# Three fp32r passes per product become one plain fp32 product, and four loading slots become ten

## Chip, cores, metric

The kernel runs on one core of one Trainium2 chip. The time is the device time in microseconds of one execution; the median of three runs stands below. One execution was also profiled. Engines are named as in the profile: PE (matrix products) with PEld (its weight loads), DVE (vector), ACT (activations), POOL, and SP, which here issues the weight transfers.

## What is computed

Two transformer-like blocks over 16 + 256 tokens of width 1024, everything in fp32. The first block has two layers:

```python
h = concat(meta_tokens, x)                              # 272 x 1024
h = layer_norm(ALPHA * h + rglru_block(h, ...))         # recurrent block, width 1344, gates 8 x 168 x 168
h = layer_norm(ALPHA * h + swiglu(h, ffn_w_in, ffn_w_out))     # 1024 -> 2 x 3584 -> 1024
h = layer_norm(ALPHA * h + gla_block(h, ...))           # gated linear attention, 4 heads
h = layer_norm(ALPHA * h + moe_swiglu(h, ...))          # top 2 of 8 experts, D_FF 3584
```

The last 256 rows go on to a second block: a modulation by a vector through `w_ada_2` (1024 x 6144), a mixed latent and differential attention (projections `w_in_2`, `w_uq_2`, `w_ukv_2`, `w_o_2`), and a mixture of 16 experts of width 512.

## The kernel before, in words

Each engine has one program, written out in order; semaphores count what is done, and a `wait_ge` names the mark. PE, ACT, DVE, POOL and SP go through: setup, recurrent block (`pe_rg`, L867), FFN (`pe_ffn`, L1107), GLA (`pe_gla`, L1256), router and first mixture (`pe_first`), second attention (`pe_mid`, L2755), router and second mixture (`pe_pairs`).

All weights outside the mixtures come in chunks of up to 128 x 2048 fp32 (1 MB), listed in a `Stream` named M in the order of use: 105 chunks before the first mixture, 16 after it. `load_chunks` (L483, issued by SP) puts chunk i into raw slot i mod 4. Most chunks are then *split*: ACT writes the part that fp32r keeps (`split_hi`, L454, the instruction at L462), DVE subtracts it from the raw chunk (`split_lo`, L474, at L480), into one of three pairs of slots. A raw slot is free again once its chunk is split (or, for chunks that PE also reads raw, used); a pair is free once PE has used it. The 24 chunks of `w_ada_2` are not split. The programs of ACT and DVE call the splits by hand, between their other work, in the order of the chunks.

Activations that are the other operand are turned by PE (transposes into PSUM) and are split too: `act_turn` and `dve_turn` (L511, L521), and where a layer norm's gain and shift belong to it, `act_shift_turn` and `dve_shift_turn` (L533, L548), which first write the value to a temporary tile, then its high part, then its low part. The key names which turn: x0, x1, x2, x3, x5, cq, x6, x6b. In the recurrent block the convolution's result and y are split in the same way (xch, xcl), in the FFN the gated value (fah, fal). A bank of PSUM goes back when the low part is written.

Every product of this kind is `mm3`:

```python
e.matmul(o, lh, rh, start=start, stop=False)     # L437
e.matmul(o, lh, rl, start=False, stop=False)     # L438
return e.matmul(o, ll, rh, start=False, stop=stop)   # L439
```

It is called in the recurrent block (`pe_rg_in`, the gates, the output), in the FFN (gate and up with the weights stationary and 272 columns streamed; down with the activations stationary and 512 columns streamed), in GLA through `pe_chan`, `pe_tokm`, `pe_rows_out` and `pe_last_two` (L1222, L1232, L1244, L642), and in `pe_mid`. Products with a raw operand are plain fp32 already: the modulation (`pe_ada`), the 16 meta rows of the down and output products (`pe_meta_rows`), GLA's small products (L1274 is one of four with 272 columns), attention, and the experts' products of both mixtures.

Both mixtures load expert weights into a ring in the memory that raw, high and low slots (10 together) held before, plus one slot (first) or three (second). `ring_slots` (L1558) gives for each slot the mark after which it is free. `load_first` (L1585) reads the expert's number from the tile perm, which the routing writes, before it issues the first load. The second mixture's order is fixed. `load_chunks` for the 16 chunks of the second attention waits until the first mixture's last use of the slot.

Of the kernel before, what the change touches and what calls it, by code (L numbers as in the profile page):

```python
# [18 lines left out]
T = 272  # L19
CW = 2048  # L20
NRAW, NSPL = 4, 3
# [98 lines left out]
class Stream:  # L120


    def __init__(self, raw, hi, lo, pe, name=""):
        self.raw, self.hi, self.lo, self.pe, self.name = raw, hi, lo, pe, name
        self.chunks, self.split, self.index, self.stop, self.kept = [], [], {}, None, set()

    def add(self, key, rows, n, pieces, split=True, zero=False, keep=False):
        i = len(self.chunks)
        if keep:
            self.kept.add(i)  # L130
        if split:
            self.split.append(i)
        self.index[key] = i
        self.chunks.append((key, rows, n, pieces, len(self.split) - 1 if split else None, zero))

    def again(self):
        for sig in (*self.raw, *((self.hi, self.lo) if self.hi is not None else ())):
            sig.n = 0


def build(nc, d, out):
# [9 lines left out]
    M = Stream([Sig(sem(f"s_raw{i}_in")) for i in range(NRAW)], Sig(sem("s_hi")), Sig(sem("s_lo")), pe)  # L151
# [4 lines left out]
    with ExitStack() as own:  # L156
        right = lambda name, shape, dt=F32: own.enter_context(nc.sbuf_tensor(name, shape, dt, side="right"))
        xh = right("xh", [128, 8, T], F32R)
        xl = right("xl", [128, 8, T], F32R)
        raw = right("raw", [128, NRAW, CW])  # L160
        whi = right("whi", [128, NSPL, CW], F32R)
        wlo = right("wlo", [128, NSPL, CW], F32R)
    with ExitStack() as own:
        xg1_ = own.enter_context(nc.sbuf_tensor("xg1", [128, 2560], F32, side="right"))
# [3 lines left out]
    ring = right("ring", [128, NRAW + 2 * NSPL, CW])  # L168
# [31 lines left out]
    def plan_ada(n):  # L200

        for _ in range(n):
            j = next(n_ada)
            part = w_ada[256 * (j % 4):256 * (j % 4) + 256, 1024 * (j // 4):1024 * (j // 4) + 1024]
            M.add(("ada", j), 128, CW, by_rows(part, 0, 2, 1024), split=False)

# [15 lines left out]
    for j in range(6):  # L222
        M.add(("ro", j), 112, CW, by_blocks(w_ro, j, 112), keep=True)
# [5 lines left out]
    for j in range(14):  # L229
        M.add(("ffn", "d", j), 128, CW, by_blocks(d["ffn_w_out"][0], j, 128), keep=True)  # L230
# [19 lines left out]
    def plan_first(S, key):  # L250
# [4 lines left out]
        def chunk(x, u, nm, gi, j):  # L255
# [9 lines left out]
            S.add((key, x, nm, gi, j, u), 128, w, pieces, split=False)  # L265
# [9 lines left out]
    first_split = len(M.split)  # L275
# [10 lines left out]
    def plan_pairs(S, key):  # L286

        rows_of = lambda w, j, m: (lambda s: [(s.rearrange("p (k n) -> p k n", k=m), w.rearrange("(p k) n -> p k n", p=128)[:, j * m:j * m + m, :])])
        for what, x in moe_order(8, 512):
            for nm, n in (("g", "w_gate_2"), ("u", "w_up_2")) if what == "u" else (("d", "w_down_2"),):  # L290
                for j in range(2):
                    for u in range(2):
                        S.add((key, x, nm, j, u), 128, CW, rows_of(d[n][0, 2 * x + u], j, 2 if nm == "d" else 4), split=False)

    R1 = Stream([Sig(sem(f"s_first{i}_in")) for i in range(NRING1)], None, None, pe, "first")
    plan_first(R1, "m1")
    R2 = Stream([Sig(sem(f"s_ring{i}_in")) for i in range(NRING)], None, None, pe, "second")
# [3 lines left out]
    class Again:  # L301


        def __init__(self, name, n_ring, plan, keys):
            self.pe, self.act, self.dve = (Sig(sem(f"s_{name}_{n}_done")) for n in ("pe", "act", "dve"))
            self.S = Stream([Sig(sem(f"s_{name}_ring{i}_in")) for i in range(n_ring)], None, None, self.pe, name)
# [38 lines left out]
    xch = ph("xch", [112, 12, T], F32R)  # L345
    xcl = ph("xcl", [112, 12, T], F32R)
# [4 lines left out]
    fah = ph("fah", [128, 28, T], F32R)  # L351
    fal = ph("fal", [128, 28, T], F32R)
    fam = ph("fam", [128, 28, 32])
# [51 lines left out]
    cq = ph("cq", [128, 2, 5, 256], F32R)  # L405
# [30 lines left out]
    def mm3(e, o, lh, ll, rh, rl, start, stop):  # L436
        e.matmul(o, lh, rh, start=start, stop=False)  # L437
        e.matmul(o, lh, rl, start=False, stop=False)  # L438
        return e.matmul(o, ll, rh, start=False, stop=stop)  # L439

    def weights(e, S, key):

        i = S.index[key]
        _, rows, n, _, s, _ = S.chunks[i]
        if s is None:
            e.wait_ge(S.raw[i % NRAW].s, S.raw[i % NRAW].at(i))
            return raw[0:rows, i % NRAW, 0:n]
        e.wait_ge(S.lo.s, S.lo.at(s))
        return whi[0:rows, s % NSPL, 0:n], wlo[0:rows, s % NSPL, 0:n]
# [4 lines left out]
    def split_hi(e, S, s):  # L454
        if s >= (len(S.split) if S.stop is None else S.stop):
            return
        i = S.split[s]
        _, rows, n, _, _, _ = S.chunks[i]
        e.wait_ge(S.raw[i % NRAW].s, S.raw[i % NRAW].at(i))
        if s >= NSPL:  # L460
            e.wait_ge(S.pe.s, S.pe.at("used", S.split[s - NSPL]))
        e.activation(whi[0:rows, s % NSPL, 0:n], raw[0:rows, i % NRAW, 0:n], ACT.Copy).then_inc(S.hi.s, S.hi.up((s,)))  # L462

    def split_half(e, S, s, half):
        i = S.split[s]
        a = slice(CW // 2 * half, CW // 2 * half + CW // 2)
        e.wait_ge(S.hi.s, S.hi.at(s))
        ins = e.tensor_tensor(wlo[:, s % NSPL, a], raw[:, i % NRAW, a], whi[:, s % NSPL, a].bitcast(F32), ALU.subtract)
        if half:
            ins.then_inc(S.lo.s, S.lo.up((s,)))  # L470
        else:
            ins.then_inc(dve.s, dve.up())

    def split_lo(e, S, s):  # L474
        if s >= (len(S.split) if S.stop is None else S.stop):
            return
        i = S.split[s]
        _, rows, n, _, _, _ = S.chunks[i]
        e.wait_ge(S.hi.s, S.hi.at(s))
        e.tensor_tensor(wlo[0:rows, s % NSPL, 0:n], raw[0:rows, i % NRAW, 0:n], whi[0:rows, s % NSPL, 0:n].bitcast(F32),  # L480
                        ALU.subtract).then_inc(S.lo.s, S.lo.up((s,)))

    def load_chunks(e, S, begin, end):  # L483

        for i in range(begin, end):
            _, rows, n, pieces, s, zero = S.chunks[i]
            k = i % NRAW
            if first <= i < first + NRAW:
                e.wait_ge(pe.s, pe.at("ring", R1.name, last_in(ring[:, 2 * NSPL + k, :])))
            if i >= NRAW:  # L490
                p = S.chunks[i - NRAW][4]
                if p is None or i - NRAW in S.kept:
                    e.wait_ge(S.pe.s, S.pe.at("used", i - NRAW))
                else:
# [3 lines left out]
            slot = raw[0:rows, k, 0:n]  # L498
# [4 lines left out]
    def pe_turn(e, key, src, tiles, nk):  # L503
        for k in range(nk):
# [4 lines left out]
            bank.give((key, k), (dve, key, "lo", k))  # L509

    def act_turn(e, key, tiles, nk, hi, gain=None):  # L511
        c0, c1 = min(c for _, _, c in tiles), max(c + n for _, n, c in tiles)
        for k in range(nk):
            p, o = bank(key, k)[:, c0:c1], hi[:, k, c0:c1]
            e.wait_ge(pe.s, pe.at(key, "T", k))
            if gain is not None and gain(k) is not None:
                e.activation(o, p, ACT.Copy, scale=gain(k)).then_inc(act.s, act.up((key, "hi", k)))
            else:
                e.activation(o, p, ACT.Copy).then_inc(act.s, act.up((key, "hi", k)))

    def dve_turn(e, key, tiles, nk, hi, lo, gain=None):  # L521
        c0, c1 = min(c for _, _, c in tiles), max(c + n for _, n, c in tiles)
        for k in range(nk):
            p, oh, ol = bank(key, k)[:, c0:c1], hi[:, k, c0:c1], lo[:, k, c0:c1]
            e.wait_ge(act.s, act.at(key, "hi", k))
            if gain is not None and gain(k) is not None:
                e.scalar_tensor_tensor(ol, p, gain(k), oh.bitcast(F32), ALU.mult, ALU.subtract).then_inc(dve.s, dve.up((key, "lo", k)))  # L527
            else:
                e.tensor_tensor(ol, p, oh.bitcast(F32), ALU.subtract).then_inc(dve.s, dve.up((key, "lo", k)))  # L529

    NTMP = 4

    def act_shift_turn(e, key, tiles, hi, gain, shift, tmp):  # L533


        c0, c1 = min(c for _, _, c in tiles), max(c + n for _, n, c in tiles)
        for k in (1, 3, 5, 7):
            x = tmp[:, k % NTMP, 0:c1 - c0]
            e.wait_ge(pe.s, pe.at(key, "T", k))
            if k >= NTMP:  # L540
                e.wait_ge(dve.s, dve.at(key, "lo", k - NTMP))
            e.activation(x, bank(key, k)[:, c0:c1], ACT.Identity, bias=shift(k), scale=gain(k)).then_inc(act.s, act.up((key, "x", k)))
            for j in (k - 1, k):
                sig = act if j % 2 else dve
                e.wait_ge(sig.s, sig.at(key, "x", j))
                e.activation(hi[:, j, c0:c1], tmp[:, j % NTMP, 0:c1 - c0], ACT.Copy).then_inc(act.s, act.up((key, "hi", j)))

    def dve_shift_turn(e, key, tiles, hi, lo, gain, shift, tmp):  # L548
        c0, c1 = min(c for _, _, c in tiles), max(c + n for _, n, c in tiles)

        def whole(k):
            e.wait_ge(pe.s, pe.at(key, "T", k))
            if k >= NTMP:
# [2783 lines left out]
```

## Time and profile before

| | us |
|---|---|
| median of 3 runs | 1938.63 (1934.21 to 1939.75) |
| the profiled execution | 1938.98 |
| its span, first to last instruction | 1936.9 |
| PE busy in it | 1812.8 (94%) |
| DVE, ACT, POOL busy | 607.6, 476.9, 351.6 |
| mean granted PE clock | 0.964 |

A span's engines overlap, so busy times don't add up. A row of PE has the time from a record's start to its modelled end; successive records overlap, and the distance of their starts is what a record costs in a stream. The granted clock is given as a share of 2.4 GHz.

### The profile page before, as it was taken

To read this page: it belongs to the slowest core of one execution; us is meant where nothing else is said; L and a number is where in the kernel's file an instruction comes from. 1 tells how busy PE (TensorE), PEld (TensorE's weight loads), DVE (VectorE), ACT (ScalarE), POOL (GpSimd) and SP (SyncE) were. 2 spreads that over 40 slices of the span, in tenths; PEclk is the share of its full clock that TensorE was granted. 3 is DMA by queue.
4 is the path that set the end of the run, shared out by engine and by line. 5 is a ranking of instruction groups with operands and counts; after the bars stand their busy time and mean duration, and the time that the engine had idled before them with its cause. 6 is when DMAs were issued, how large, how long until landed. Compare 5 with 4: busy or idle time off the path is not lost.

```text
span 1936.9 us, 26926 instructions
## 1 busy us (share of the span) xinstructions
PE 1812.8 (94%) x11141; PEld 1033.9 (53%) x11141; DVE 607.6 (31%) x1227; ACT 476.9 (25%) x799; POOL 351.6 (18%) x306
## 2 busy tenths in 40 slices
PE   7999999999998999999999999999997887699998
PEld 7987999777975333323332333222322886544443
DVE  6777554338466200100010000000001685501112
ACT  5854444325332110000100000000001564321121
POOL 3000000000000699999930000000000000000000
PEclk9998999998998899999999999999999897889999
DMA  6555667446724999999999999999998440569997
GB/s 192 150 146 187 202 199 241 142 141 220 249 89 155 402 418 413 420 419 420 413 419 420 419 412 416 420 419 419 415 420 297 137 158 9 217 275 417 420 420 291
DMA packets 152739, 582.87 MB, mean 301 GB/s; under 512 B 11673, under 2 KB 77866, under 8 KB 109600
## 3 DMA queue, kind: packets, MB, share of 16 engines
q1 hardware_dynamic: 150000, 575.09, 76.4%
q0 software_dynamic: 2608, 5.97, 1.2%
q8 instruction: 91, 1.49, 0.3%
q14 instruction: 40, 0.33, 0.1%
HBM read 579.96 MB, written 1.05 MB: 300 GB/s over the span
## 4 chain that ended last, share of the span: by engine, by line
PE 73%; DMA 14%; DVE 8%; ACT 3%; issue 1%; SPq 0%; ACTq 0%; DVEq 0%
PE ps L1789 17%; DMA ring<-in_moe_w_out 9%; PE ps L437 9%; PE ps L438 8%; PE ps L439 8%; PE ps L2294 6%; PE ps L1782 5%; PE ps L1821 4%; PE ps L2318 3%; DMA ring<-in_moe_w_in 3%; DVE wlo L480 2%; DMA more<-in_moe_w_out 1%; PE ps L1825 1%; DMA more<-in_moe_w_in 1%; PE ps L637 1%
## 5 line engine op out<-in xcount | busy, mean ns | idle before, releaser
L1789 PE MATMUL ps<-ring,xg 128*64 128x512 f32 x1638 | 406.3, 599 | 4.5 <-DMA ring<-in_moe_w_in 2.4
L480 DVE TENSOR_TENSOR wlo<-raw,whi 128x2048 fp32r<-128x2048 f32 (+5 forms) x96 | 211.5, 2207 | 190.0 <-ACT whi L462 189.7
L1789 PEld LDWEIGHTS ps<-ring,xg 128*64 128x64 f32 x1638 | 120.9, 137 | 247.5 <-issue 239.6
L462 ACT ACTIVATE whi<-raw 128x2048 fp32r<-128x2048 f32 (+6 forms) x97 | 178.7, 1846 | 184.7 <-PE ps L439 77.5
L1821 PE MATMUL ps<-ring,ahm 128*64 128x512 f32 x808 | 203.4, 597 | 8.4 <-DMA ring<-in_moe_w_out 8.4
L437 PE MATMUL ps<-xh,whi 128*128 128x272 f32 (+1 forms) x712 | 210.6, 296 | 0.6 <-DVE xl L529 0.6
L439 PE MATMUL ps<-xh,wlo 128*128 128x272 f32 (+1 forms) x712 | 208.8, 293 | 0.0
L438 PE MATMUL ps<-xl,whi 128*128 128x272 f32 (+1 forms) x712 | 208.6, 293 | 0.0
L2219 POOL TENSOR_SCALAR lnt<-lnt,h 128x384 f32<-128x384 f32 x120 | 188.6, 1572 | 12.2
L1962 DVE TENSOR_TENSOR sgm<-sgm,ps 128x512 f32<-128x512 f32 x28 | 17.5, 683 | 495.7 <-PE ps L1789 495.7
L437 PEld LDWEIGHTS ps<-xh,whi 128*128 128x128 f32 (+1 forms) x712 | 133.7, 188 | 4.0 <-issue 2.4
L438 PEld LDWEIGHTS ps<-xl,whi 128*128 128x128 f32 (+1 forms) x712 | 133.8, 188 | 0.5
L439 PEld LDWEIGHTS ps<-xh,wlo 128*128 128x128 f32 (+1 forms) x712 | 133.5, 187 | 0.5
L1821 PEld LDWEIGHTS ps<-ring,ahm 128*64 128x64 f32 x808 | 63.4, 136 | 131.4 <-issue 131.4
L2221 POOL TENSOR_TENSOR bias<-bias,lnt 128x384 f32<-128x384 f32 x120 | 120.2, 1002 | 10.0
L437 PE MATMUL ps<-whi,xh 128*128 128x256 f32 (+3 forms) x368 | 112.2, 305 | 3.3 <-DVE xl L527 1.6
L438 PE MATMUL ps<-wlo,xh 128*128 128x256 f32 (+3 forms) x368 | 111.1, 302 | 0.0
L439 PE MATMUL ps<-whi,xl 128*128 128x256 f32 (+3 forms) x368 | 110.9, 301 | 0.0
L1782 PE MATMUL ps<-ring,xg 128*32 128x384 f32 (+1 forms) x936 | 106.4, 554 | 2.7 <-DMA ring<-in_moe_w_in 2.3
L2294 PE MATMUL ps<-ring,xg 128*64 128x512 f32 x392 | 100.0, 608 | 1.6 <-ACT xg L2358 1.6
L2517 POOL DMA_DIRECT2D gbr<-in_mla_q_g x1 | 0.5, 547 | 511.4 <-ACT kk L2721 511.4
L1972 DVE SCALAR_TENSOR_TENSOR yl<-ps,gs,yh 128x512 fp32r<-128x512 f32 x8 | 5.6, 747 | 271.0 <-ACT yh L1910 271.0
(586 smaller groups left out, 2439.8 us busy)
## 6 DMA issues: line engine op xcount, KB each, us to landing
ring<-in_moe_w_in SPq DMA_DIRECT2D x117, 1024.0 KB, 19.6
ring<-in_moe_w_out SPq DMA_DIRECT2D x101, 1024.0 KB, 20.1
ring<-in_moe_w_in SPq DMA_DIRECT2D x117, 768.0 KB, 11.9
ring<-in_w_gate SPq DMA_DIRECT2D x29, 1024.0 KB, 14.2
raw<-in_ffn_w_in SPq DMA_DIRECT2D x28, 1024.0 KB
ring<-in_w_down SPq DMA_DIRECT2D x26, 1024.0 KB, 12.9
raw<-in_w_ada SPq DMA_DIRECT2D x24, 1024.0 KB
ring<-in_w_up SPq DMA_DIRECT2D x20, 1024.0 KB, 9.9
```

The costliest lines, as they stand in the source:

```text
L437: e.matmul(o, lh, rh, start=start, stop=False)
L438: e.matmul(o, lh, rl, start=False, stop=False)
L439: return e.matmul(o, ll, rh, start=False, stop=stop)
L462: e.activation(whi[0:rows, s % NSPL, 0:n], raw[0:rows, i % NRAW, 0:n], ACT.Copy).then_inc(S.hi.s, S.hi.up((s,)))
L480: e.tensor_tensor(wlo[0:rows, s % NSPL, 0:n], raw[0:rows, i % NRAW, 0:n], whi[0:rows, s % NSPL, 0:n].bitcast(F32), ALU.subtract).then_inc( ...
L1782: ins = e.matmul(po[32 * c:32 * c + 32, 0:n // 4], a[:, j, 128:160], quarter(both[0][:, 0, :], n, c), start=j == 0, stop=j == 7)
L1789: ins = e.matmul(ps_[b][64 * v:64 * v + 64, :], a[:, j, 64 * v:64 * v + 64], both[v][:, 0, 512 * b:512 * b + 512], start=j == 0, stop=j == 7)
L1821: ins = e.matmul(D[q][64 * v:64 * v + 64, :], w["ahm"][:, f, 64 * v:64 * v + 64], both[v][:, i, 512 * q:512 * q + 512], start=f == 0, stop ...
L2219: e.tensor_scalar(stp[:, :], rel[:, :], float(th), dl[:, i, hh:hh + 1], ALU.is_ge, ALU.mult).then_inc(pool.s, pool.up())
L2221: e.tensor_tensor(bias[:, hh, :], bias[:, hh, :], stp[:, :], ALU.add).then_inc(pool.s, pool.up())
L2294: ins = e.matmul(p[64 * v:64 * v + 64, :], xg[:, kk_, u + 64 * v:u + 64 * v + 64], both[v][:, k, :], start=kk_ == 0, stop=kk_ == 7)
L2318: ins = e.matmul(D[q][64 * v:64 * v + 64, :], w["ah"][:, x % 2, f, 64 * v:64 * v + 64], both[v][:, i, 512 * q:512 * q + 512], start=f == 0 ...
```

## The change

`mm3`, `split_hi`, `split_lo`, `split_half` and the shift turns are gone. Every product that was `mm3` is one `e.matmul` on fp32 tiles; the chunks are used where they land. The stream M has ten slots (the ring's own) in place of four; a slot is free when PE has used its chunk. xh is the tile xg, xl is gone; cq, fa, X2 and I are used unsplit. A turn is shared: DVE writes the even k, ACT the odd, each in one instruction with gain and shift, and a bank goes back at that mark. `ring_slots` takes an order of the last ten chunks. POOL's four memsets for the gates' chunks wait for nothing. The router's products, the mixtures and the attention inside are as they were.

```diff
-NRAW, NSPL = 4, 3
+NRAW = 10
...
-    ring = right("ring", [128, NRAW + 2 * NSPL, CW])
+    ring = right("ring", [128, NRAW, CW])
+    xh = xg
...
     def load_chunks(e, S, begin, end):
...
             if first <= i < first + NRAW:
-                e.wait_ge(pe.s, pe.at("ring", R1.name, last_in(ring[:, 2 * NSPL + k, :])))
+                e.wait_ge(pe.s, pe.at("ring", R1.name, last_in(ring[:, k, :])))
             if i >= NRAW:
-                p = S.chunks[i - NRAW][4]
-                if p is None or i - NRAW in S.kept:
-                    e.wait_ge(S.pe.s, S.pe.at("used", i - NRAW))
-                else:
-                    e.wait_ge(S.lo.s, S.lo.at(p))
+                e.wait_ge(S.pe.s, S.pe.at("used", i - NRAW))
...
+    def dve_turn(e, key, tiles, nk, to, gain=None, shift=None):
         c0, c1 = min(c for _, _, c in tiles), max(c + n for _, n, c in tiles)
+        for k in range(0, nk, 2):
+            p, o = bank(key, k)[:, c0:c1], to[:, k, c0:c1]
+            e.wait_ge(pe.s, pe.at(key, "T", k))
+            if shift is not None:
+                e.tensor_scalar(o, p, gain(k), shift(k), ALU.mult, ALU.add).then_inc(dve.s, dve.up((key, "x", k)))
...
                     for k in range(8):
                         if j == 0 and nm == "g" and i == 0:
-                            e.wait_ge(dve.s, dve.at("x1", "lo", k))
-                        ins = mm3(e, p, wh[:, k, 128 * i:128 * i + 128], wl[:, k, 128 * i:128 * i + 128], xh[:, k, :], xl[:, k, :],
-                                  k == 0, k == 7)
+                            wait_x(e, "x1", k)
+                        ins = e.matmul(p, w[:, k, 128 * i:128 * i + 128], xh[:, k, :], start=k == 0, stop=k == 7)
...
-                e.tensor_tensor(g, g, bank("fu", f)[:, 0:T], ALU.mult).then_inc(dve.s, dve.up(("fu", f)))
-                e.wait_ge(act.s, act.at("fa", f))
-                e.tensor_tensor(fal[:, f, :], g, fah[:, f, :].bitcast(F32), ALU.subtract).then_inc(dve.s, dve.up())
-                e.tensor_copy(fam[:, f, :], g[:, 0:32]).then_inc(dve.s, dve.up(("fa", f)))
+                e.tensor_tensor(fa[:, f, :], g, bank("fu", f)[:, 0:T], ALU.mult).then_inc(dve.s, dve.up(("fu", f), ("fa", f)))
...
+    LAST1 = chunk_at(*(("ada", j) for j in (16, 17, 18)), ("go", 2), ("go", 3), *(("ada", j) for j in range(19, 24)))
+    LAST2 = list(range(len(M.chunks) - NRAW, len(M.chunks)))
+    SLOTS1 = ring_slots(LAST1, [more1[:, i, :] for i in range(NMORE1)], "end_gla")
```

## Rows read from the trace of the kernel before

**Rows 1.** The page, chain of waits by engine, whole span
```profile
PE 73%; DMA 14%; DVE 8%; ACT 3%; issue 1%; SPq 0%; ACTq 0%; DVEq 0%
```

**Rows 2.** Windows by stage: us, busy (instructions) of each engine, PEclk, DMA share, GB/s
```profile
0.00:620.00 620.00, 592.19 (x4337) 514.53 (x4337) 367.86 (x618) 270.40 (x354) 23.28 (x38) 0.97 0.55 179
620.00:1500.00 880.00, 832.84 (x4631) 274.85 (x4632) 72.65 (x209) 60.17 (x122) 320.64 (x257) 0.98 1.00 408
1500.00:1702.00 202.00, 160.08 (x1009) 144.43 (x1007) 133.09 (x337) 100.37 (x220) 7.67 (x12) 0.84 0.38 125
1702.00:1936.90 234.90, 227.70 (x1166) 100.14 (x1166) 34.01 (x66) 45.96 (x106) 0.00 (x0) 0.99 0.91 376
```

**Rows 3.** Groups of PE by form, line L437 (busy us, mean ns)
```profile
L437 PE MATMUL ps<-xh,whi 128*128 128x272 f32 x512 | 151.1, 295 | 0.0
...
L437 PE MATMUL ps<-whi,xh 128*128 128x256 f32 x256 | 72.5, 283 | 0.9 <-ACT row L613 0.9
...
L437 PE MATMUL ps<-xh,whi 128*112 128x272 f32 x192 | 56.3, 293 | 0.6 <-DVE xl L529 0.6
...
L437 PE MATMUL ps<-whi,fah 128*128 128x512 f32 x112 | 45.4, 405 | 0.0
...
L437 PE MATMUL ps<-whi,xh 128*128 128x512 f32 x64 | 26.2, 410 | 1.8 <-DVE xl L527 1.6 <-DVE xl L529 0.2
...
L437 PE MATMUL ps<-whi,xch 112*128 112x512 f32 x48 | 19.4, 404 | 0.0
...
L437 PE MATMUL ps<-xch,whi 112*112 112x272 f32 x56 | 17.0, 303 | 2.2 <-ACT R L928 2.2
```

**Rows 4.** PE timeline at three places: start us, duration us
```profile
299.91 0.29 PE L437 MATMUL ps<-xh,whi 128*128 128x272 f32 x1
...
301.81 0.29 PE L437 MATMUL ps<-xh,whi 128*128 128x272 f32 x1
...
539.91 0.27 PE L437 MATMUL ps<-whi,xh 128*128 128x256 f32 x1
...
541.33 0.28 PE L437 MATMUL ps<-whi,xh 128*128 128x256 f32 x1
...
149.86 0.39 PE L437 MATMUL ps<-whi,xch 112*128 112x512 f32 x1
...
151.24 0.39 PE L437 MATMUL ps<-whi,xch 112*128 112x512 f32 x1
```

**Rows 5.** Plain fp32: source line L1274; then weight loads of L2274, timeline
```profile
L1274 PE MATMUL ps<-zT,h x8: 387/388/463, 461.4 to 463.0; 16*128 16x272 f32 x8
...
1816.12 0.19 PEld L2274 LDWEIGHTS ps<-h,cst 128*128 128x128 f32 x1 [0.24 <-issue]
...
1818.27 0.19 PEld L2274 LDWEIGHTS ps<-h,cst 128*128 128x128 f32 x1 [0.24 <-issue]
```

**Rows 6.** Window of the gates stage, columns as in rows 2
```profile
56.10:80.90 24.80, 22.64 (x168) 22.41 (x168) 18.73 (x42) 19.11 (x32) 0.00 (x0) 0.93 0.42 120
```

**Rows 7.** Who PE waited for: us in total, times, longest us
```profile
PE ps L437 <- DVE wlo L480: 4.1, 2, 3.5
...
PE ps L2637 <- ACT Sx L2629: 2.8, 2, 2.5
...
PE ps L437 <- ACT R L928: 2.2, 1, 2.2
...
PE ps L730 <- DVE xl L560: 1.7, 2, 0.8
```

**Rows 8.** DVE timeline before the first softmax
```profile
1589.78 4.49 DVE L480 TENSOR_TENSOR wlo<-raw,whi 128x2048 fp32r<-128x2048 f32 x2
```

**Rows 9.** SP's queue, 600 to 640 us
```profile
624.96 6.21 SPq L1601 DMA_DIRECT2D ring<-in_moe_w_in  x10
```

**Rows 10.** PE timeline, GLA's outputs: start us, us, records
```profile
557.03 0.70 PE L1323 MATMUL ps<-vt,sc 128*128 128x256 f32 x2
557.66 0.65 PE L1325 MATMUL ps<-Sst,E 128*64 128x256 f32 x4
```

More of the change, by code:

```diff
@@ L120, with __init__, add @@
 class Stream:
[L123 to L134, printed above, removed]
+    def __init__(self, raw, pe, name=""):
+        self.raw, self.pe, self.name = raw, pe, name
+        self.chunks, self.index = [], {}
+    def add(self, key, rows, n, pieces, zero=False):
+        self.index[key] = len(self.chunks)
+        self.chunks.append((key, rows, n, pieces, zero))
     def again(self):
-        for sig in (*self.raw, *((self.hi, self.lo) if self.hi is not None else ())):
+        for sig in self.raw:
             sig.n = 0
@@ L150, in build @@
         "posr", "relb", "small", "br", "out")}
-    M = Stream([Sig(sem(f"s_raw{i}_in")) for i in range(NRAW)], Sig(sem("s_hi")), Sig(sem("s_lo")), pe)
+    M = Stream([Sig(sem(f"s_raw{i}_in")) for i in range(NRAW)], pe)
     cst = sb("cst", [128, C_END])
[L156 to L162, printed above, removed]
     with ExitStack() as own:
@@ L433, in build @@
     phase_ctx[0].close()
[L436 to L439, printed above, removed]
     def weights(e, S, key):
         i = S.index[key]
[L444 to L449, printed above, removed]
+        _, rows, n, _, _ = S.chunks[i]
@@ L451, in used @@
+        e.wait_ge(S.raw[i % NRAW].s, S.raw[i % NRAW].at(i))
+        return ring[0:rows, i % NRAW, 0:n]
     def used(S, key):
         return ("used", S.index[key])
[L454 to L470, printed above, removed]
-        else:
[L472 to L481, printed above, removed]
@@ L496, in load_chunks @@
             if zero:
                 e.wait_ge(pool.s, pool.at("zero", i))
-            slot = raw[0:rows, k, 0:n]
+            slot = ring[0:rows, k, 0:n]
             for dst, src in pieces(slot):
@@ L508, in pe_turn, with act_turn @@
             ins.then_inc(pe.s, pe.up((key, "T", k)))
-            bank.give((key, k), (dve, key, "lo", k))
-    def act_turn(e, key, tiles, nk, hi, gain=None):
+            bank.give((key, k), by_turns(key, k))
+    def act_turn(e, key, tiles, nk, to, gain=None, shift=None):
         c0, c1 = min(c for _, _, c in tiles), max(c + n for _, n, c in tiles)
-        for k in range(nk):
-            p, o = bank(key, k)[:, c0:c1], hi[:, k, c0:c1]
+        for k in range(1, nk, 2):
+            p, o = bank(key, k)[:, c0:c1], to[:, k, c0:c1]
@@ L531, in build @@
[L531 to L546, printed above, removed]
@@ L709, in by_turns, with wait_x, pe_turn_tiles @@
         return (act if k % 2 else dve, key, "x", k)
-    def act_router_turn(e, key, gain, shift):
-        for k in range(1, 8, 2):
-            e.wait_ge(pe.s, pe.at(key, "T", k))
-            e.activation(xg[:, k, 0:256], bank(key, k)[:, 0:256], ACT.Identity, bias=shift(k), scale=gain(k)).then_inc(
-                act.s, act.up((key, "x", k)))
-    def dve_router_turn(e, key, gain, shift):
-        for k in range(0, 8, 2):
-            e.wait_ge(pe.s, pe.at(key, "T", k))
-            e.tensor_scalar(xg[:, k, 0:256], bank(key, k)[:, 0:256], gain(k), shift(k), ALU.mult, ALU.add).then_inc(
-                dve.s, dve.up((key, "x", k)))
-    def pe_turn_tiles(e, key, norm, tiles, nk, ahead, back=None):
+    def wait_x(e, key, k):
+        sig, *mark = by_turns(key, k)
+        e.wait_ge(sig.s, sig.at(*mark))
+    def pe_turn_tiles(e, key, norm, tiles, nk, ahead):
         p = {}
@@ L741, in pe_turn_tiles @@
             e.transpose(p[k][:, c:c + n], src_h(t, k), idn[0:n, 0:n]).then_inc(pe.s, pe.up((key, "T", k)))
-            bank.give((key, k), (dve, key, "lo", k) if back is None else back(key, k))
+            bank.give((key, k), by_turns(key, k))
     def pool_ln(e, i, *after):
@@ L798, in pool_setup @@
             i = M.index["gt", j]
-            p = M.chunks[i - NRAW][4]
-            if p is None:
-                e.wait_ge(pe.s, pe.at("used", i - NRAW))
-            else:
-                e.wait_ge(M.lo.s, M.lo.at(p))
-            e.memset(raw[0:112, i % NRAW, 0:2016], 0.0).then_inc(pool.s, pool.up(("zero", i)))
+            e.memset(ring[0:112, i % NRAW, 0:2016], 0.0).then_inc(pool.s, pool.up(("zero", i)))
     def pe_setup(e):
@@ L1153, in act_ffn @@
         for j in range(14):
-            for _ in range(2):
-                split_hi(e, M, s)
-                s += 1
             for f in (2 * j, 2 * j + 1):
@@ L1179, in dve_ffn @@
         for j in range(14):
-            for _ in range(2):
-                split_lo(e, M, s)
-                s += 1
             for f in (2 * j, 2 * j + 1):
@@ L1470, in dve_gla @@
         dve_ada(e, 3)
-        for j in range(6):
-            split_lo(e, M, s)
-            s += 1
         for ch in range(4):
@@ L2223, in pool_rel @@
         pool.label(("round_m1",))
-    SLOTS = ring_slots("wo", len(M.chunks), [more[:, i, :] for i in range(2)], "end_mid") + [(xslot[:, 0:CW], ((pe, "m2", "logits"),))]
+    SLOTS = ring_slots(LAST2, [more[:, i, :] for i in range(2)], "end_mid") + [(xslot[:, 0:CW], ((pe, "m2", "logits"),))]
     NP = 8
@@ L2772, in pe_mid @@
                 for k in range(3):
[L2773 removed]
+                    ins = e.matmul(p[:, 0:384], cq[:, k, cc:cc + 128], w[:, k, :], start=k == 0, stop=k == 2)
                 ins.then_inc(pe.s, pe.up(("uq", j, t), used(M, ("uq", j))))
                 bank.give(("uq", j, t), (act, "uq", j, t))
[L2776 removed]
+        w = weights(e, M, ("ukv", 0)).rearrange("p (k n) -> p k n", k=2)
         for t, _, cc in QTILES:
@@ L3039, in dve_mid @@
         dve_angles(e)
-        for j in range(3):
-            split_lo(e, M, s)
-            s += 1
         for t in range(2):
```

417 lines of the change are left out of this document (105 added, 312 removed).

## The prediction

> **What bounds the kernel now.** I read first the chain of waits: PE carries 73% of it and the DMA 14% [rows 1], so PE is the first suspect. The windows by stage [rows 2] then say where. Up to 620 us (recurrent block, first FFN, GLA) PE is busy 592.2 of 620 us at a mean clock of 0.97, while the DMA stands at 0.55, DVE at 368 us and ACT at 270 us: this stage is PE's, and splitting is beside it. From 620 to 1500 (first mixture) the DMA share is 1.00 at 408 GB/s: that stage is the DMA's. From 1500 to 1702 (second attention) PE is busy 160 of 202 us at clock 0.84: a stage of handovers between engines. The second mixture follows. The edited products lie in the first and third window only, and there PE's own rate is what the edit changes.
>
> **Counts.** A product of three passes is one record each at L437, L438 and L439. The forms of L437 [rows 3] give 512 + 192 + 56 products that stream 272 columns and 8 more for gz, so 768; 256 that stream 256 columns, and by the code 32 more with a 16-wide stationary tile (gv, tile 2); 112 + 64 + 48 that stream 512, and by the code 8 more (ukv), so 232; by the code 12 of 384 columns (uq) and 16 of 160 (wi 8).
>
> **The price of a pass now.** Durations overlap, so I take starts, not durations. 272 columns: from 299.91 to 301.81 there are 15 steps of 0.127 us; 256: from 539.91 to 541.33, 12 steps of 0.118; 512: from 149.86 to 151.24, 6 steps of 0.230 [rows 4]. A product costs three: 0.380, 0.354 and 0.690 us.
>
> **The price of a plain fp32 product.** The trace has some. At L1274 the code has four products of 272 columns and the row has 8 records: a plain product is two records. They start in 1.6 us for 7 steps, 0.229 each. At L2274, with a full 128x128 stationary tile and 512 columns, the weight loads start from 1816.12 to 1818.27 in 5 steps of 0.430 [rows 5]. Between the two it is 0.84 ns per column, 2 cycles of 2.4 GHz; so 256 columns give 0.216 and 384 give 0.322 per record. A plain product then costs 0.458 (272), 0.432 (256), 0.860 (512). It is one third fewer records, but each streams at half the rate.
>
> The Trainium skill, "FP8 and Floating Point Precision", TensorE Precision Notes, says that true fp32 takes four passes through the array, a reduced read of fp32 one. The trace agrees: 0.860 us for 512 columns is 4.03 cycles per column. A second rule speaks louder against the change: "TensorE: Matmul & The Clock Gate", Back-to-back issue gap, gives columns/2.4 + 2.5 ns for a pass, which would be 116 ns for 272 columns where the trace has 127. By it the three passes would cost 0.347, 0.328 and 0.648 us and the added PE time would be some 164 us in place of the 123 below. Of the passes that run now the measurement decides.
>
> **Added on PE.** 768 x 0.078 = 59.9; 288 x 0.078 = 22.5; 232 x 0.170 = 39.4; 12 of 384 columns, interpolated, 12 x 0.12 = 1.5; the 16 of 160 columns: bounds -1 (by columns) and +1 (the 256-column difference), taken as 0. Sum +123.3 us. It falls in stages where PE is the limit, so all of it is on the path, unless waits disappear.
>
> **What comes off.**
> - The splits themselves (L462 on ACT, L480 on DVE) and the second half of every turned operand: beside PE's work nearly everywhere (DVE busy 368 of 620 us), so worth only the waits below.
> - Gates, 56.1 to 80.9: 168 records at 0.127 would take 21.3, the stretch took 24.8 [rows 6]; ACT came late there behind splits (PE waited 2.2 for ACT R L928 [rows 7]). Minus 3.5.
> - x1 and x2: PE waited 1.7 us in two waits for DVE xl L560, which gives banks back [rows 7]; now the turned value itself does. Minus 1.7. What ends these turns next is the norm itself (DVE, then ACT), which stays.
> - ukv: PE waited 3.5 us for DVE wlo L480 [rows 7]; with ten slots its weights lie ready. Minus 3.5, and minus 1.8 because those 24 records then run warm: between 0, if they stay cold, and 1.8.
> - Attention: two splits held DVE 4.49 us from 1589.78 [rows 8], just before the first softmax; ACT's two are similar. Bounds 0 (if PE's scores end later anyway) and 4.5. PE's longest wait for the softmax (ACT Sx L2629) was 2.5 [rows 7]; ACT's backlog delays the heads' copies before it too, so I take minus 3.7, nearer to the upper end. What is late next is ACT's row of exponentials.
> - The low halves of x at the first product, at x6b and at the x3 turn, and ACT's ada rows late behind splits: minus 3.6 together, between 0 and 5 (an estimate: four to five handovers like the two of x1 and x2, at 0.85 each).
> - Against it: where the granted clock is 1.2 GHz a pass of 272 columns takes 272/1.2 = 0.227, and the difference of a product is one pass, 0.227, not 0.078. Bounds 0 and 5 (ten such stretches, half a microsecond each), taken as 2.
>
> Sum of these: -3.5 - 1.7 - 5.3 - 3.7 - 3.6 + 2 = -15.8.
>
> **Ten loading slots.** In the first stage a 1 MB chunk feeds 16 products, 7.3 us after the change, at a DMA share of 0.55 now: no wait to win. The ring's first expert loads are issued at 624.96 [rows 9], after the routing's perm (load_first reads it), in both kernels; free slots earlier change nothing. After the first mixture the first loads of the second block now wait for the last two expert chunks, since slot 5 is the one used next to last; PE then has a norm to wait for and eight transposes ahead of wi 0, a product set of 16 lasts 6.9 us (16 x 0.432), and a chunk of 1 MB lands each 2.6 us at 408 GB/s [rows 2]: cost 0, and 5 at the most, two chunks' landing. The 13 slots of the second mixture come free before it in both kernels, the last at the router's logits: 0. POOL's memsets lose a wait and hold nobody. The 0.078 per product also delays nothing else: DVE, ACT and SP follow PE here.
>
> **Forecast.** Span 1936.9, the execution 1938.98, so 2.1 us lie around the span. 1938.98 + 123.3 - 15.8 = 2046.5; the median of the runs is 1938.63, 0.3 lower. I say **2046 us**, about 5.5% slower.
>
> **Rivals.**
> - *Weight loads come out from behind the streams.* At L1323 two plain records of 256 columns take 0.63 us until the next line starts, 0.315 each where 0.216 was priced: 0.10 more [rows 10]. If every new record paid that, 2 x 1316 x 0.10 = +263, so 2310. It decides as soon as a load cannot start under the stream before it. Against it: at L2274 six loads of the same size are hidden in a stream, and L1323 alternates with 64-wide tiles. If the plain streams only carry the excess that the passes of 272 have over their columns (127 against 113, so 14 ns), it is 2632 x 0.014 = +37: 2083. Chance 0.06 for the small form, 0.02 for the full one.
> - *Faster: a plain record streams as a pass does.* Two records of 0.127 in place of three: 768 x 0.127 + 288 x 0.118 + 232 x 0.23 = -185, with the waits about 1740. It decides below a record of 1.5 passes, 0.190 us for 272 columns. Rows 5 speak against it with 0.229 measured; only a difference between these few products and the new ones could save it. Chance 0.02.
> - *PE's longer stage is hidden by the DMA.* The expert loads would have to start before 620; up to 11 chunks of 2.6 us are 28 us, which gives 2018. Rows 9 and the read of perm speak against it. Chance 0.03.
> - *The waits hold more than I took off.* PE's idle time up to 620 is 28 us and in the third window 42 [rows 2], most of it norms and softmax. If another 15 go: 2031. Inside the forecast's range. Chance of the forecast with this: 0.87.
>
> **Range and chances.** 2028 takes in all bounds of waits (another 8) and half of the last rival; 2068 takes in no gain from attention and ukv (+9), the cold bound (+3) and a third of the 14 ns excess. About 0.3% is what a measurement of this kernel can tell from no change. Faster comes from the second rival, 0.02; same has no mechanism of its own, a partial sum of several, 0.01; slower 0.97.
>
> **What would show it.** Right: one matmul line in place of three, with two records per product; starts 0.229 apart at 272 columns and 0.43 at 512; the FFN's gate and up part (448 products) about 35 us longer, the window of the first mixture 880 us as before, only later; no PE wait on ukv. Wrong: spacings over 0.24 at 272 columns, PE waits on DMA for weights before 620, expert loads issued before the routing, or a first mixture that is shorter.

## The result and the profile after

The changed kernel takes **2036.73 us** (median of 4 runs, 2034.33 to 2038.59) where the kernel before takes 1937.86 beside it: a ratio of 1.0512, 95% interval 1.0492 to 1.0531, or 99 us more. The forecast was 2046, range 2028 to 2068. The direction and its cause, dearer products on the engine that sets the pace, hold. The 99 are not made of the terms that I summed, though: I had +123.3 on PE and -15.8 beside it, and the profiled spans differ by 95.3 (1936.9 and 2032.2), so some 28 us came back, not 15.8.

The page of the changed kernel, busy time by engine and the chain of waits by engine (before: [rows 1]):

```profile
PE 1923.1 (95%) x9825; PEld 971.9 (48%) x9825; DVE 363.3 (18%) x1011; ACT 279.9 (14%) x611; POOL 350.2 (17%) x306
...
PE 81%; DMA 13%; DVE 4%; ACT 1%; issue 1%; SPq 0%; ACTq 0%; DVEq 0%
```

PE carries 81% of the chain instead of 73%; DVE falls from 8% to 4%. The windows of the changed kernel, columns as in [rows 2], here cut at the changed kernel's own stage ends (first stage, first mixture, second attention, and the gates alone):

```profile
0.00:703.00 703.00, 683.40 (x3099) 460.85 (x3099) 150.73 (x395) 98.00 (x187) 23.00 (x38) 0.98 0.49 157
703.00:1582.00 879.00, 838.61 (x4721) 275.79 (x4720) 74.42 (x224) 60.26 (x118) 316.48 (x250) 0.98 0.98 403
1582.00:1798.00 216.00, 173.92 (x840) 135.36 (x840) 104.18 (x326) 75.75 (x201) 10.71 (x18) 0.89 0.41 137
63.16:88.83 25.67, 25.67 (x113) 19.82 (x112) 8.54 (x32) 13.26 (x26) 0.00 (x0) 1.00 0.52 154
```

The whole loss is in the first window. The same two instructions, the first record of GLA's last ada rows ahead of the routing, start at 606.56 before and at 703.10 after, 96.5 us apart; the end of the last mixture's records moves by 95.3. The mixture only starts later, and in the second attention, where the products add some 18 us (128 x 0.078, 40 x 0.17 and 1.5), nearly all of it is given back.

The price of a plain product, from the critical chain of the changed kernel (start us, us, what; each row is one unbroken series of records):

```profile
239.37 29.44 PE ps L921 x128
269.81 29.53 PE ps L921 x128
...
506.41 13.95 PE ps L561 x32
...
574.39 21.20 PE ps L1020 x96
```

L921 (FFN gate and up, 272 columns), L561 (512) and L1020 (256) are the priced forms. With the last record's own duration taken off (0.395, 0.595 and 0.382 us, the means of their groups) the steps are (29.53 - 0.395) / 127 = 0.229, 13.36 / 31 = 0.431 and 20.82 / 95 = 0.219 us. I had priced 0.229, 0.430 and 0.216 from eight records and six weight loads of another part of the kernel [rows 5].

Who PE waited for, changed kernel (us in total, times, longest us):

```profile
PE ps L450 <- ACT hn L2273: 9.5, 1, 9.5
...
PE ps L638 <- ACT h L609: 6.2, 3, 2.6
...
PE ps L2377 <- ACT Sx L2369: 1.0, 3, 0.4
```

No wait on split weights is left, since there are none. Ahead of the x1, x2 and router turns (L638) PE now waits for the norm instead of for banks.

### The profile page after: what moved, and what is told of

It is laid out like the page before. It is cut to its first block, busy times and chain, and to the rows that moved or that the text cites. A ratio compares the mean times of both kernels' runs of the same rounds, so it can differ in the third digit from the quotient of the medians.

```text
span 2032.2 us, 23789 instructions
## 1 busy us (share of the span) xinstructions
PE 1923.1 (95%) x9825; PEld 971.9 (48%) x9825; DVE 363.3 (18%) x1011; ACT 279.9 (14%) x611; POOL 350.2 (17%) x306
## 4 chain that ended last, share of the span: by engine, by line
PE 81%; DMA 13%; DVE 4%; ACT 1%; issue 1%; SPq 0%; ACTq 0%; DVEq 0%
PE ps L1533 16%; PE ps L921 10%; DMA ring<-in_moe_w_out 9%; PE ps L1020 6%; PE ps L2037 6%; PE ps L1565 4%; PE ps L745 4%; PE ps L1526 4%; PE ps L942 4%; PE ps L2061 3%; PE ps L561 3%; DMA ring<-in_moe_w_in 3%; PE ps L1008 2%; PE ps L776 1%; PE ps L761 1%; PE ps L1569 1%
## 5 line engine op out<-in xcount | busy, mean ns | idle before, releaser
L921 PE MATMUL ps<-xg,ring 128*128 128x272 f32 x896 | 208.5, 395 | 0.0
L921 PEld LDWEIGHTS ps<-xg,ring 128*128 128x128 f32 x896 | 170.5, 191 | 36.9 <-issue 2.1
L1020 PE MATMUL ps<-ring,xg 128*128 128x256 f32 (+2 forms) x608 | 131.6, 377 | 0.0
L1020 PEld LDWEIGHTS ps<-ring,xg 128*128 128x128 f32 (+1 forms) x608 | 107.8, 181 | 23.3 <-issue 3.2
L745 PE MATMUL ps<-xg,ring 128*112 128x272 f32 x384 | 90.6, 399 | 0.0
L942 PE MATMUL ps<-ring,fa 128*128 128x512 f32 x192 | 85.6, 599 | 0.0
L745 PEld LDWEIGHTS ps<-xg,ring 128*112 128x112 f32 x384 | 69.2, 181 | 20.7
L1533 PE MATMUL ps<-more,xg 128*64 128x512 f32 x154 | 70.5, 597 | 1.2 <-DVE sgm L1706 0.9
L1569 PE MATMUL ps<-ring,aho 128*32 128x512 f32 x400 | 52.4, 602 | 5.5 <-DMA ring<-in_moe_w_out 4.1
L942 PEld LDWEIGHTS ps<-ring,fa 128*128 128x128 f32 x192 | 35.5, 190 | 45.1 <-issue 45.1
```

The costliest lines, as they stand in the source:

```text
L745: ins = e.matmul(p, w[:, k, 112 * i:112 * i + 112], xh[:, k, :], start=k == 0, stop=k == 7)
L921: ins = e.matmul(p, w[:, k, 128 * i:128 * i + 128], xh[:, k, :], start=k == 0, stop=k == 7)
L942: e.matmul(acc[t, q][0:n, :], fa[:, f, cc:cc + n], w[:, i, 512 * q:512 * q + 512], start=f == 0, stop=False)
L1020: ins = e.matmul(p, xh[:, k, cc:cc + nt], w[:, k, :], start=k == 0, stop=k == 7)
L1533: ins = e.matmul(ps_[b][64 * v:64 * v + 64, :], a[:, j, 64 * v:64 * v + 64], both[v][:, 0, 512 * b:512 * b + 512], start=j == 0, stop=j == 7)
L1569: ins = e.matmul(Do[32 * c:32 * c + 32, :], w["aho"][:, 2 * j + i, :], both[0][:, i, 512 * q:512 * q + 512], start=j == 0, stop=j == 13)
```

## The experiments

Each ran beside the kernel before; ratios are to it. Spans quoted are those of the profiled executions.

**1. Plain products, but every split kept.** From the kernel before:

```diff
     def mm3(e, o, lh, ll, rh, rl, start, stop):
-        e.matmul(o, lh, rh, start=start, stop=False)
-        e.matmul(o, lh, rl, start=False, stop=False)
-        return e.matmul(o, ll, rh, start=False, stop=stop)
+        return e.matmul(o, lh.bitcast(F32), rh.bitcast(F32), start=start, stop=stop)
```

> The kernel before, its splits, its four loading slots and all their waits kept, but each product is one plain fp32 product of the two high parts (both products with a low part are left out, so less is computed). Theory (the passes cost +123 us on PE, and what the change gives back comes from the splits alone): the passes' +123 us stay whole, and most of the 28 us that the change gave back stay out, so 1938 + 123 = 2061 us, or down to 2050 where slower products cover some split waits. Rival (the 28 us come from PE itself, as from a better clock, or from the slots): the same 2037 us as the changed kernel if from the product's form, since the splits cost nothing.

Measured: 2044.94 us, 1.0576 (1.0558 to 1.0593); span 2040.5. Below my theory's range (2050 to 2061) and above the rival's value (2037). Taking away all the splitting, sharing the turns and adding six slots is worth together the 8.3 us between its span and the changed kernel's. So of some 28 us that come back, about 20 come back with every split still in place. The gates show how (window of the gates in this run):

```profile
64.57:90.32 25.75, 25.75 (x114) 19.74 (x113) 17.45 (x38) 19.06 (x32) 0.00 (x0) 1.00 0.43 135
```

ACT still works 19.06 us here, as before [rows 6], and PE no longer waits: it takes 25.75 us with the splits and 25.67 without. It was not the splits' going that removed this wait. PE became slower than what it had waited for. The clock is part of it too: 1.00 in this window, 0.93 before [rows 6]. Of the wait on split weights (3.5 us ahead of ukv in [rows 7]) only 0.8 us is left, although each weight is still split.

**2. Fewer slots filled ahead.** The changed kernel with the loads held back, to six, seven or eight chunks:

```diff
             if i >= NRAW:
-                e.wait_ge(S.pe.s, S.pe.at("used", i - NRAW))
+                e.wait_ge(S.pe.s, S.pe.at("used", i - 6))
```

> The changed kernel, but each load waits until the chunk six places earlier has been used, so that at most six of the ten slots are filled ahead. Theory (the number of slots brings nothing: a 1 MB chunk feeds PE for 3.5 us or more and 2.6 us suffice to land one): 2037 us, within 1.5 us. Rival (the ten slots carry part of the 28 us that the change gave back): slower by 3 us or more, with PE waiting for the ring's loads in the dense stages.

Measured: 2046.95 us, 1.0575 (1.0555 to 1.0595). My theory fell: slots matter. The row for it, from who PE waited for:

```profile
PE ps L509 <- DMA ring<-in_w_ada: 10.4, 4, 4.8
```

All four waits lie in one place, at the end of GLA, where the stream has five chunks of w_ada close together and PE takes 1.9 us for each. Held back to four chunks the program stops, each engine waiting for another, so there is no time for that; where the circle closes was not looked into. To see whether the kernel before would have been as short of slots (it had four raw and three split ones), seven and eight:

> The changed kernel with loads at most seven chunks ahead (four loading slots plus three split ones were seven). With six, PE waited 10.4 us for w_ada chunks of the ring around 660 to 710 us, where five of them follow each other and PE needs only 1.9 us for each. Theory A (the kernel before had enough depth for this run of short chunks, so the ten slots bring nothing over it): 2037 to 2039 us, without those waits. Theory B (each slot less costs one landing in that run of chunks): 2041 to 2044 us, some 5 to 8 us of waits for w_ada left.

> The changed kernel with loads at most eight chunks ahead. Theory A: as with ten, 2037 us. Theory B: 2038 to 2041 us, between seven and ten.

Measured: seven 2043.96 us, 1.0554 (1.0538 to 1.0570), with this row:

```profile
PE ps L509 <- DMA ring<-in_w_ada: 4.7, 2, 3.5
```

Eight: 2040.43 us, 1.0539 (1.0523 to 1.0555), one such wait of 2.6 us. Both medians agree with theory B. In the traces the first part of the first mixture starts 10.7 (six), 7.6 (seven) and 4.0 us (eight) later than with ten. SP's queue in this stretch suggests why. First the kernel with seven, 650 to 730 us (who the queue waited for), then its issues of w_ada (start us, us, count) and, last, those of run 1 in its own stretch:

```profile
SPq L443 <- PE ps L561: 14.5, 1, 14.5
```

```profile
664.93 39.21 SPq L443 DMA_DIRECT2D ring<-in_w_ada  x6
```

```profile
658.53 51.09 SPq L498 DMA_DIRECT2D raw<-in_w_ada  x7
```

Without splits a loading slot is held until the last product of its chunk, and L561 reads two chunks of go for 14 us. With seven slots one load of w_ada stands 14.5 us behind it. The kernel before needed no more than seven, since its split freed the raw slot before PE read the copy (lines 491 to 495 wait for the split). That last step is read from the code, not shown by a run. In run 1, too, one load of w_ada stands 14.5 us behind a wait for PE, without making PE wait. What the traces do show is that PE has no wait on w_ada, neither in the kernel before nor in run 1, both with four raw slots and three pairs. So ten slots gain nothing over the kernel before, but they are part of the price of taking the split away: with seven in all, the change costs 7 us more.

**3. Two splits moved.** The kernel before, three passes, with the second and third wo chunk split after the first softmax step, not ahead of it (DVE's half; ACT's likewise):

```diff
-        for _ in range(2):
-            split_lo(e, M, s)
-            s += 1
         dve_scores(e, 0)
...
         dve_scores(e, 2)
+        split_lo(e, M, s)
         dve_values(e, 0)
...
         dve_probs(e, 2)
+        split_lo(e, M, s + 1)
+        s += 2
         dve_values(e, 2)
```

> The kernel before, three passes kept; only the splits of the second and third chunk of wo are moved out of the time before the first softmax: ACT's after the second group's head copies and before the last group's exponentials, DVE's before the first and the third group's value sums. Theory (the attention gave back 7.9 us because these four splits stood ahead of the softmax): 4 to 8 us faster than the kernel before, 1930 to 1934 us, with the stretch from the last of wi to the first product of wo shorter by that. Rival (PE's other waits, or the slower head copies, set that stretch): 1938 us, within 1 us; or slower, if the later splits now delay the value sums or wo.

Measured: 1932.12 us, 0.9979 (0.9967 to 0.9991), 3 to 4 us less than before: the right way, at the lower edge of the 4 to 8 expected. Its twelve runs lie between 1926.76 and 1936.21 us, and the time goes with the mean granted clock of the run: the three at 0.964 took 1934.8 to 1935.8, the four at 0.969 took 1926.8 to 1929.0. The profiled one took 1935.32. The chain of the kernel before (start us, us) shows what was moved, with what stood on DVE's path up to the softmax:

```profile
1581.85 2.20 DVE wlo L480
1584.05 2.27 DVE rs L3074 x2
...
1588.56 1.22 DVE pj L3080
1589.87 4.40 DVE wlo L480 x2
1594.27 2.61 DVE Sx L2618 x8
1596.90 1.82 DVE ssum L2622 x2
1598.75 1.04 ACT Sx L2629 x5
```

From the first head turn to wo's first product the kernel before takes 1641.13 - 1585.53 = 55.60 us, this one 49.67, so 5.9 less (2.2 of it is lost again between GLA and the x5 turn, in the first mixture above all); the changed kernel takes 47.76, 7.8 less. But run 1, with all splits where they were, takes 46.85, less than any of them. Something else is in that stretch. The starts of the same instructions, in us after the first head turn, and the mean granted clock from it to wo, show where:

| | first transpose of exponentials | first value product | next scores | wo | clock |
|---|---|---|---|---|---|
| before | 14.35 | 23.79 | 31.50 | 55.60 | 0.79 |
| experiment 3 | 10.09 | 18.69 | 25.60 | 49.67 | 0.87 |
| changed kernel | 10.10 | 18.69 | 25.77 | 47.76 | 0.89 |
| run 1 | 11.76 | 20.36 | 24.40 | 46.85 | 0.96 |

Up to the first value product, moving the splits and having none are worth the same. Run 1 keeps them and is ahead of the kernel before by 2.6 us at the first transpose: the slower products already cover part of the splits. After the value products it overtakes the others. The granted clock is the difference there: windows of PE (us, busy, clock, DMA share, GB/s) around those 24 value products and the 12 transposes behind them, in the kernel before, the changed kernel and run 1:

```profile
1609.32:1617.10 7.78, 7.78 (x39) 0.50 0.00 0
```

```profile
1705.39:1712.54 7.15, 7.15 (x40) 0.55 0.00 0
```

```profile
1713.53:1717.64 4.11, 4.11 (x40) 1.00 0.00 0
```

In the kernel before PE worked only 6.5 of the 10 us from 1590 on, behind the softmax; from 1600 on its clock was 0.60 and then 0.50, which is 1.2 GHz:

```profile
1590.00:1600.00 10.00, 6.50 (x41) 1.00 0.59 209
1600.00:1605.00 5.00, 4.10 (x20) 0.60 0.02 5
1605.00:1610.00 5.00, 4.21 (x22) 0.50 0.00 0
```

Those records, on the path, ran at that level before, nearly all of them in the changed kernel too, and at 2.4 GHz in run 1. Why the clock stayed up in run 1 is not shown: PE worked 3.29 and 2.80 us of the two stretches of 5 us from 1705 on, no more than the 3.19 and 2.81 us of those from 1598 on in experiment 3, where the clock then fell.

**4. PE kept busy where it waits.** Experiment 3 with transposes of the identity ahead of PE's waits in the attention, into banks that the next product overwrites (they add nothing to any result):

```diff
+    def fill(e, p, n):
+        for _ in range(n):
+            e.transpose(p[:, 0:128], idn, idn)
...
         bk = [bank.take(e, "values", B, t) for t in range(2)]
+        fill(e, bk[0], (0, 0, 36, 18)[B])
```

> The kernel with the two moved wo splits, and transposes of the identity added where PE idles in the attention (3 ahead of each score product of the second group, 5 ahead of each of the first group's transposes of the exponentials, 16 ahead of the last group's head turns, 36 and 18 ahead of the third and the last group's value products), into banks that the next product overwrites. Theory (in the run that kept the splits but had single plain products, the attention came out 5 us shorter from the first exponentials to the x6 turn than in the kernel before, because its granted clock stayed at 1.00 where that of the others fell to 0.50): the clock stays high from 1600 to 1640, and the kernel comes out 3 to 8 us below the one with moved splits, 1924 to 1929 us. Rival (the clock falls anyway, or the softmax on ACT and DVE sets every step and hides the cold products): within 1 us of it, or some tenths slower by the added transposes.

Measured: 1925.42 us, 0.9944 (0.9928 to 0.9961). PE's windows of experiment 3 and of this one:

```profile
1590.00:1640.00 50.00, 38.86 (x257) 0.86 0.15 49
```

```profile
1590.00:1640.00 50.00, 47.41 (x371) 1.00 0.13 43
```

The clock stays at 1.00 and the stretch from the first head turn to wo falls to 45.22 us, another 4.4, although the added transposes delay its first value product by 1.7 us (20.44 after the first head turn, 18.69 in experiment 3). So the clock was that second thing. The median is 6.7 us below experiment 3's; the 2.3 beyond this stretch lie in parts that were not edited. In the profiled executions 1.1 of it stands at the x7 turn, where the clock came out higher; the rest has no cause shown. The Trainium skill, "TensorE: Matmul & The Clock Gate", Part 1: The HAM clock gate, says that the engine runs at half its clock after it has idled and at the full one once it is kept busy; here the clock fell behind idle time in experiment 3 and held at 1.00 once PE was kept busy, and work without a use will do. Run 1, idle as much before its value products and at 1.00, shows that idle time does not always bring it down.

**5. The same at the other long waits**: ahead of the gates, of the x1, x2, x3, x5 and x7 turns and of ukv.

```diff
+        p0 = bank.take(e, "ukv", 0, 0)
+        fill(e, p0, 30)
         wh, wl = (w.rearrange("p (k n) -> p k n", k=2) for w in weights(e, M, ("ukv", 0)))
```

> The kernel of the run e5_warm (three passes, moved wo splits, PE kept busy in the attention) with transposes of the identity also where PE waits ahead of the gates, of the x1, x2, x3, x5 and x7 turns and of ukv. In e5_warm the granted clock was below 0.9 at 166 to 176, 449 to 459, 578 to 584, 1497 to 1518 and 1557 to 1563 us, some 45 us in all of which PE was busy for about 35 and on the path for about 25. Theory (cold products on the path cost up to their warm time again): 6 to 13 us below e5_warm, 1912 to 1919 us, with a granted clock of 1.00 there. Rival (the norms on ACT and DVE set the turns, and the added transposes delay what they stand ahead of): within 2 us of e5_warm, to either side.

Measured: **1920.05 us, 0.9915 (0.9902 to 0.9929)**, 16 us below the kernel before and some 116 below the changed one, with the arithmetic of three passes unchanged. That is 5 us better than run 4, just short of the 6 to 13 expected. At x1 the clock rose only in part:

```profile
160.00:178.00 18.00, 13.88 (x70) 0.72 0.83 289
```

```profile
160.00:178.00 18.00, 15.98 (x105) 0.91 0.82 289
```

(run 4, then this one). The turn itself took 9.63 us from the last product before it to the first one behind it in both, since the norm on ACT and DVE sets when PE may go on; 1.0 us came from the products behind it. The gates gave 1.5, ukv 1.6, the x7 turn 1.1. Ahead of x5 the clock stood at 0.90 instead of 0.66 and 1.3 us came of it.

**6. Two passes.** The kernel before without its third product (low part of the left operand by high part of the right one):

```diff
         e.matmul(o, lh, rh, start=start, stop=False)
-        e.matmul(o, lh, rl, start=False, stop=False)
-        return e.matmul(o, ll, rh, start=False, stop=stop)
+        return e.matmul(o, lh, rl, start=False, stop=stop)
```

> The kernel before with the third product (low part of the left operand by the high part of the right one) left out, all splits, slots and waits kept. Theory (PE bounds the dense stages, DVE and ACT follow at half their time): one pass comes off each of some 1300 products, 768 x 0.127 + 288 x 0.118 + 232 x 0.230 + 12 x 0.17 = 187 us, of which new split and load waits give back 10 to 40: 1760 to 1790 us. Rival (the splits are near the bound already: DVE 2.4 us a chunk and ACT 1.9 beside the operand turns): waits take half of it, 1840 us or more.

Measured: 1822.91 us, 0.9421 (0.9407 to 0.9434), 112 us off, not 145 to 175. It lies between theory and rival: some 75 of the 187 us that leave PE come back, 68 in the profiled executions. Outside the mixtures PE idles 122.6 us where it idled 70.2 before, so 52 of the 68 are waits. The rest is about what the clock costs: PE is busy at the lower level for 102.5 us there, before for 73.0, and the same work at that level takes nearly twice as long (an estimate: some 15 us). Some of the waits on ACT and DVE there:

```profile
PE ps L437 <- DVE wlo L479: 30.2, 12, 7.4
...
PE ps L729 <- ACT h L699: 9.5, 2, 5.6
...
PE ps L437 <- ACT lnt L952: 6.6, 1, 6.6
PE ps L437 <- ACT R L927: 5.2, 1, 5.2
PE ps L437 <- DVE modc L626: 5.2, 1, 5.2
```

With a third of the passes gone the splits do become the bound in places, 30.2 us of it on the low halves of weights (4.1 before [rows 7], 0.8 in run 1). Runs 1 and 6 are the two sides of one statement: what the splits cost depends on how long PE takes for a chunk.

## Why the prediction was right, and where not

**The PE term held.** +123.3 us were priced; the steps came out at 0.229, 0.431 and 0.219. Over the FFN's gate and up part (448 products) the start of the same instructions moved by 57.3 - 22.9 = 34.4 us, where 448 x 0.078 = 34.9; over its down part (112 products, the last 16 at L561 included) 18.4 for 19.0. At that 1 to 3% less the term is some 121. The first rival, loads coming out from behind the streams, is dead: weight loads of L921 take 0.19 us and the records still start every 0.229.

**Of the two rules of the Trainium skill** the one on fp32's four passes ("FP8 and Floating Point Precision", TensorE Precision Notes) agrees once more: 0.431 us for 512 columns is 4.04 cycles per column and product. By the gap rule ("TensorE: Matmul & The Clock Gate", Back-to-back issue gap), which its section gives for a single product without the load of its weights, the estimate was +164. The forecast with the trace's own spacings was nearer, by the 0.127 us that a pass of 272 columns really took.

**Gates, -3.5: right in size, wrong in cause.** The stretch grew by 25.67 - 24.80 = 0.9 where the products alone add 56 x 0.078 = 4.4, so 3.5 came off. I wrote that ACT came late behind splits. Run 1 keeps them and takes 25.75: the longer products cover the 2.2 us of waiting, and the clock is 1.00 instead of 0.93.

**ukv, -5.3:** from the first uq to wi 5 the stretch went from 17.17 to 14.61 us, where uq and ukv add 1.5 + 1.4: 5.5 off. Run 1, with the splits, has 15.64, so 4.4 of the 5.5 come with slower products and a warm clock, and 1.0 with the splits gone.

**x1 and x2, -1.7:** about 1.4, none of it in run 1, so this one does belong to the turns without splits. The banks come back early, and the norm on ACT is what PE waits for next, as said (L638, 6.2 us).

**Attention, -3.7: the mis-sized step.** It gave 7.8. Two terms were taken for one. Up to the first transpose of the exponentials the changed kernel gains 4.3 us (14.35 to 10.10), as experiment 3 does by moving the splits; run 1 gets 2.6 of it with the splits in place. The rest comes behind that, where more of PE's work runs at the higher level. The clock I had booked only as a cost ("where the granted clock is 1.2 GHz", +2), and never asked whether the changed order of waits would raise it. It did: 0.79 to 0.89 from the first head turn to wo. The +2 had the right price: at 1.2 GHz the steps of 272 columns are 0.227 us for a pass and 0.454 for a plain record. But only 27 records of the edited products, some 14 products, start at that level in the changed kernel, where 91 records, some 30 products, did before.

**The small waits, -3.6:** the first product came 0.7 earlier and the x3 turn gave 1.5; the x7 turn, which I hadn't in the list, another 1.2; wo with the x6b turn inside it gave 1.7. The two mixtures and x5 were 2 us shorter in this profile, about what the DMA-bound part differs by from run to run (run 3's was 2.3 longer than before's), so I claim nothing for them.

**Slots: a right number for a wrong reason.** "No wait to win" against the kernel before holds. But I argued from the mean DMA share and from chunks that feed PE 7.3 us, and so missed the one place with short chunks; there fewer than ten slots cost 4 to 11 us.

**The same account by kind.** The items above are by place. By kind it reads so, for the two stages that hold the edited products (up to the first routing, and from the end of the first mixture to the second routing; us of PE):

| | length | idle | busy at 1.2 GHz |
|---|---|---|---|
| before | 814.9 | 70.2 | 73.0 |
| run 1 | 919.7 | 63.4 | 42.8 |
| changed kernel | 911.8 | 57.3 | 42.5 |

Idle time fell by 7 us with the slower products alone and by 6 more without the splits. The time at the lower level fell by 30 in both, and that is worth 11 to 15 us (an estimate: a plain record takes twice as long there, a pass of 272 columns 0.227 in place of 0.127). So about half of what came back is clock, a term that my sum didn't have, and all of that half comes with the form of the product and none with the splits. The range held because the PE term is so much larger than the others; the small terms together were short by some 10 us, most of it clock. These are single executions, but the mean granted clock bears them out: 0.970 to 0.974 in every run of run 1's kernel and of the changed one, 0.963 to 0.968 in those of the kernel before beside them.

**The range's ends.** The parts that I named for them add up to 2030 and 2070, not 2028 and 2068; nothing hangs on it.

What stays open: the items by place add up to 23 us, 25 with the mixtures, of some 26. Why the granted clock fell less often with plain products is not shown. Whether the splits and the slots, taken off apart, make exactly the 8.3 us that run 1 shows was not tried; no kernel with plain products and splits had ten slots.

## What to carry to other kernels

Price both forms of a product by the step between starts, in this program, before weighing what a cheaper form saves elsewhere: three passes at 0.127 beat two records at 0.229, and nothing that hid behind PE could win that back. A wait on a helper engine can disappear when the bound engine slows down, so a gain found there isn't a gain of removing the helper's work; keep the helper's work and change only the bound engine to tell the two apart. Count idle time and time at the lower clock separately, since either can be what came back. And where PE waits some microseconds in a chain of handovers, first move work that no one needs yet out of that chain, then look at the granted clock of the products behind the wait.

## What the runs showed of the hardware

The clock was worth more than the one handover that was moved: transposes without a use in PE's waits brought 1932 to 1925 us in one stage and 1920 over all, with the window of 50 us going from 0.86 to 1.00; the moved splits had brought 3 to 4. The same 24 value products and 12 transposes took 7.78 us at 0.50 and 4.11 at 1.00. The added work was transposes alone, so transposes keep the clock up too. Between runs of one and the same kernel the mean granted clock differed by 0.005 and the time by 9 us (experiment 3). A plain fp32 record with a new 128 x 128 stationary tile each time hides its load all but for some 0.006 us at 256 columns (0.219 us per record where its columns make 0.213; load 0.18), where a pass of 256 columns needs 0.118 instead of the 0.107 that its columns make at 2.4 GHz.
